# Expert queries of a PEER layer: one fp32 product each from the weights as loaded, in place of three products of high and low parts

## The chip, the cores and the metric

The program runs on one core of a Trainium2 chip. Its engines work side by side from their own instruction queues: TensorE (PE) multiplies, VectorE (DVE) and ScalarE (ACT) do elementwise work, GpSimd (POOL) issues the indirect gathers, SyncE (SP) issues the plain loads; semaphores join them. The metric is device microseconds of one execution; lower is better. All tensors are fp32.

## The reference, cut to what matters

Two transformer blocks on 256 tokens of width 1024. The change touches the last layer, an expert layer with 16384 experts, two tables of 1024-wide rows (`u`, `v`), 8 heads and 16 experts per head and token.

```
q = (h @ w_q).reshape(B, S, PEER_HEADS, 2, PEER_KEY_DIM)          # 1024 x 2048 weights
sc = jnp.einsum('bshpd,phnd->bshpn', q, keys)                     # 2 x 128 scores per head
v1, i1 = lax.top_k(sc[..., 0, :], 16);  v2, i2 = lax.top_k(sc[..., 1, :], 16)
...                                                               # best 16 of the 256 sums -> idx, gates
ue = jnp.take(u, it, axis=0)                                      # gathered rows of u
act = jax.nn.gelu(jnp.einsum('tkd,td->tk', ue, ht), approximate=False)
ve = jnp.take(v, it, axis=0)
return jnp.einsum('tk,tkd->td', gt * act, ve)
```

## The kernel before

**Weights.** Each matrix is cut into pieces of 1 MB, in the order of use (`weight_plan`). SP loads them into four places RAW. For each piece ACT (`hi`, L1214) writes the high part WH, rounded to fp32r, and DVE (`lo`, L1716) writes the low part WL = RAW - WH, 128x2048, and then the place in RAW may be loaded again. PE multiplies in fp32r: high by high, high by low, low by high (`mm3`). The last eight pieces are the query weights, one per head (`peer_q`). The activations, too, stand as XH and XL. `W`, `YY` and `WH`/`WL` are buffers of split weights.

**The end of the mixer.** `out_half(0, ..)` ends the first 128 tokens; DVE scales them (L2292), PE turns them round (L1082), ACT and DVE write XH and XL (`turn_half`). Then PE runs `query`: the queries of head 0 for half 0 (`first_query(0, 0)`: 16 pairs of a 128x128 weight tile and 128 columns, three products each), their scores, the rest of `out_half(1, ..)`, head 1 for half 0, and then half 1 of both heads. Heads 2 to 7 come as `query_tile(i, r)`, with all 256 tokens as columns: two tiles of 8 pairs each.

**The experts.** A "unit" is one head of one half of the tokens: its 16 experts are 16 "items" (256 in all). For item j, POOL issues a gather of 128 rows of `u` (one per token), and for item j - 8 one of `v` (512 gathers of 512 KB, L2612). DVE multiplies a u row with the token and sums (the "dot", L2451); every 8 items ACT takes the gelu and DVE the gate; ACT makes a diagonal matrix of 128 weights (L1674), PE multiplies it with the v rows and adds up in PSUM (two products of 512 columns, `item`). DVE's choice of the next unit's experts (`choose`, L2298 to L2404) lies between the dots.

**Slots.** The gathers land in 33 slots (`spots`) used in a ring: 13 at first, 12 more from item 64, 8 in RAW, two per place, as the places come free of the query weights ("lo" of pieces 4 to 7). `OPEN` says at which item a slot joins and what POOL waits for; later fills wait for the dot or the product (`v_mm`) that read the slot. `SCHEDULE` is one list that all engines follow: it says after which items a tile, the copy of its queries (`evict`), its scores, the copy of these (`keep`) and, in the kernel before, a `lo` come.

Of the kernel before, what the change touches and what calls it, by code (L numbers as in the profile page):

```python
# [126 lines left out]
def body(nc, ctx, A, out):  # L127
# [32 lines left out]
    NT = (XH[:, :, :], XL[:, :, :])  # L160
    ident, ones, negtri, negones, tri_le, tri_gt, bt_le, bt_gt = [cst[:, i, :] for i in range(8)]
# [127 lines left out]
    spots += [GS[:, i, :] for i in range(8, 20)]  # L289
    spots += [RAW[:, i // 2, D * (i % 2):D * (i % 2) + D] for i in range(8)]  # L290
# [16 lines left out]
    NSPLIT = len(plan) - 1  # L307
# [26 lines left out]
    SCHEDULE = [("query", 0), ("tile", (2, 0)), ("tile", (2, 1)), ("items", range(0, 5)), ("lo", 2), ("items", range(5, 7)),  # L334
                ("lo", 3), ("items", range(7, 8)), ("evict", 2), ("scores", 2), ("items", range(8, 9)), ("keep", 2)]
    j = 9
    for i in range(3, 8):
        t = 12 + 10 * (i - 3)
# [6 lines left out]
    Q = first["peer_q"] - 1  # L345
    OPEN = {s: (0, ("out1", 4 if s < 8 else 1)) for s in range(EARLY)}
# [15 lines left out]
    for j in range(256 + LAG):  # L362
        ring.extendleft(sorted((s for s in OPEN if OPEN[s][0] == j), key=lambda s: (s < 8, s), reverse=True))
# [24 lines left out]

    def pe_program():
# [684 lines left out]
        def turn_half(half):  # L1076
            for q in range(2):
# [7 lines left out]
                freed[i] = (S["turned"], 4 * TURN["peer"] + 2 * half + q + 1)  # L1085
# [40 lines left out]
        def query():  # L1126
            b01 = ring(0, 1)
            pe.wait_ge(S["xn"], 4)
            w0 = piece(8, ("pq_mm", 3))
# [5 lines left out]
            w1 = piece(8, ("pq_mm", 4))  # L1135
# [66 lines left out]
    def act_program():  # L1202
# [375 lines left out]
        def turn_half(half):  # L1578
            for q in range(2):
                act.wait_ge(pe.own, pe.nth("tr_half", 2 * half + q + 1))  # L1580
                nc.scalar.activation(XH[:, 4 * q:4 * q + 4, half * 128:half * 128 + 128],
                                     four(bank[at_bank["turn_half", half, q]]), ACT.Copy).then_inc(act.own, act.mark("tr_half"))
# [16 lines left out]
        hi()  # L1599
# [34 lines left out]
        def evict(i):  # L1634
# [4 lines left out]
            if i + 2 < 8:  # L1639
                hi()  # L1640
# [1063 lines left out]
```

## Time and profile before

| | us |
|---|---|
| runs | 1665.99 median (1664.35 to 1671.23, 3 runs) |
| profiled execution | 1665.4 |
| its span, first to last instruction | 1663.9 |
| first gather issued | 976.81 |
| last gather issued | 1643.61 |
| PE, DVE, ACT, POOL busy | 90%, 64%, 39%, 33% of the span |

The profiled execution is 1.5 us longer than its span, and 0.6 us under the median of the runs. The gathers move 268.47 MB of the 431.95 MB in the last 41% of the span. There the 16 DMA engines are busy nearly all the time, PE has long stretches in which it waits for data, and DVE is full only at the start. A share of busy time over the whole span says little here; the stretches are read one by one.

### The profile page before, as it was taken

What the parts mean: (1) busy time and instruction counts of PE and PEld (TensorE: products, weight loads), DVE (VectorE), ACT (ScalarE), POOL (GpSimd) and SP (SyncE); (2) the same over time, 40 slices, a digit from 0 to 9 for tenths busy, and PEclk for the clock granted to TensorE, in tenths of its full rate; (3) what the DMA queues carried; (4) which work ended last, traced back from release to release, by engine and by line L of the source; (5) the groups of instructions that cost most, each with busy time, mean ns of one, the idle gap of its engine ahead of it and who ended that gap; (6) DMA issues with size and microseconds to landing.
All of it is one profiled execution on the core that took longest, in us unless ns stands there. A gap on an engine that the chain in (4) does not pass through costs nothing.

```text
span 1663.9 us, 20481 instructions
## 1 busy us (share of the span) xinstructions
PE 1490.9 (90%) x8043; PEld 1100.5 (66%) x8043; DVE 1060.9 (64%) x1889; ACT 643.6 (39%) x1016; POOL 552.2 (33%) x607
## 2 busy tenths in 40 slices
PE   7999999999999999999999999998777777777776
PEld 7999898888888899998889886644222222222222
DVE  4655655677675555556655769776666667666655
ACT  5444343787354444444553534322222212222211
POOL 1000000311000000000010046777777776777774
PEclk9999999999999999999999999999999999999999
DMA  8555545334344355566444469999999999999997
GB/s 293 178 178 193 187 152 177 102 102 152 115 154 149 129 187 192 178 189 199 132 127 138 154 239 365 385 412 412 411 412 411 411 412 381 412 411 412 411 411 319
DMA packets 199945, 431.95 MB, mean 260 GB/s; under 512 B 20773, under 2 KB 114090, under 8 KB 199850
## 3 DMA queue, kind: packets, MB, share of 16 engines
q0 software_dynamic: 73728, 268.47, 40.5%
q1 hardware_dynamic: 123456, 159.92, 29.6%
q10 hardware_dynamic: 2666, 2.26, 0.5%
q8 instruction: 64, 1.05, 0.3%
q14 instruction: 31, 0.25, 0.0%
HBM read 429.55 MB, written 1.05 MB: 259 GB/s over the span
## 4 chain that ended last, share of the span: by engine, by line
PE 52%; POOL 17%; DVE 10%; DMA 9%; issue 7%; ACT 5%; ACTq 0%; DVEq 0%; POOLq 0%
PE ps L407 52%; POOL GS L2612 10%; POOL RAW L2612 5%; DVE WL L1716 3%; DMA GS<-in_peer_v_dram,AR 2%; ACT WH L1214 2%; DMA AR<-in_peer_v_dram,AR 2%; POOL AR L2612 2%; DMA RAW<-in_peer_v_dram,AR 2%; DMA RAW<-in_peer_u_dram,AR 1%; DMA GS<-in_peer_u_dram,AR 1%; DVE H L1758 1%; DVE XN L1753 1%; DVE XL L1772 1%; DVE AR L1980 0%
## 5 line engine op out<-in xcount | busy, mean ns | idle before, releaser
L1716 DVE TENSOR_TENSOR WL<-RAW,WH 128x2048 fp32r<-128x2048 f32 x143 | 327.9, 2293 | 232.1 <-ACT WH L1214 231.5
L407 PE MATMUL ps<-XH,WH 128*128 128x256 f32 (+1 forms) x1448 | 418.8, 289 | 12.3 <-DVE XL L1772 5.1
L407 PE MATMUL ps<-XL,WH 128*128 128x256 f32 (+1 forms) x1448 | 411.0, 284 | 0.0
L407 PE MATMUL ps<-XH,WL 128*128 128x256 f32 (+1 forms) x1448 | 410.9, 284 | 0.0
L407 PE MATMUL ps<-GS,AR 128*128 128x512 f32 x576 | 281.3, 612 | 81.4 <-DMA GS<-in_peer_v_dram,AR 70.3
L1214 ACT ACTIVATE WH<-RAW 128x2048 fp32r<-128x2048 f32 x137 | 262.4, 1915 | 181.7 <-PE ps L407 179.9
L407 PEld LDWEIGHTS ps<-XH,WH 128*128 128x128 f32 x1448 | 279.4, 193 | 21.0 <-issue 9.5
L407 PEld LDWEIGHTS ps<-XL,WH 128*128 128x128 f32 x1448 | 279.5, 193 | 3.2 <-issue 2.4
L407 PEld LDWEIGHTS ps<-XH,WL 128*128 128x128 f32 x1448 | 279.5, 193 | 0.0
L407 PEld LDWEIGHTS ps<-GS,AR 128*128 128x128 f32 x576 | 99.2, 190 | 259.5 <-issue 223.7
L2451 DVE CUSTOM_DVE_ANT_0 GS<-GS,ps 128x1024 f32<-128x1024 f32 x146 | 177.8, 1218 | 124.6 <-DMA GS<-in_peer_u_dram,AR 124.2
L2502 POOL TENSOR_TENSOR small<-small 128x1 f32<-128x1 f32 x28 | 15.4, 556 | 702.6 <-DVE small L1748 365.8
L407 PE MATMUL ps<-WH,YY 128*128 128x512 f32 x544 | 169.2, 392 | 1.6 <-DVE YY L1823 0.7
L2612 POOL DMA_INDIRECT GS<-in_peer_v_dram,AR x147 | 141.6, 963 | 45.5 <-issue 42.0
L2612 POOL DMA_INDIRECT GS<-in_peer_u_dram,AR x146 | 139.3, 954 | 51.4 <-issue 32.8
L407 PE MATMUL ps<-RAW,AR 128*128 128x512 f32 x248 | 119.5, 607 | 29.7 <-DMA RAW<-in_peer_v_dram,AR 25.5
L407 PE MATMUL ps<-AR 128*128 128x512 f32 (+8 forms) x556 | 125.6, 384 | 21.1 <-DMA AR<-in_peer_v_dram,AR 13.7
L407 PEld LDWEIGHTS ps<-AR 128*128 128x128 f32 (+3 forms) x556 | 73.4, 185 | 67.4 <-issue 48.5
L407 PEld LDWEIGHTS ps<-WH,YY 128*128 128x128 f32 x544 | 100.3, 188 | 22.7 <-issue 1.9
L1684 ACT ACTIVATE AR<-AR 128x8 f32<-128x8 f32 x32 | 6.7, 210 | 280.5 <-DVE AR L2451 280.5
L2451 DVE CUSTOM_DVE_ANT_0 RAW<-RAW,ps 128x1024 f32<-128x1024 f32 x62 | 75.4, 1217 | 54.2 <-DMA RAW<-in_peer_u_dram,AR 54.2
L407 PEld LDWEIGHTS ps<-RAW,AR 128*128 128x128 f32 x248 | 42.5, 189 | 101.4 <-issue 88.3
(372 smaller groups left out, 1988.9 us busy)
## 6 DMA issues: line engine op xcount, KB each, us to landing
RAW<-in_ffn_w_gu_dram SPq DMA_DIRECT2D x44, 1024.0 KB, 5.1
RAW<-in_w_in_dram SPq DMA_DIRECT2D x39, 1024.0 KB, 5.2
RAW<-in_ffn_w_down_dram SPq DMA_DIRECT2D x22, 1024.0 KB, 4.9
RAW<-in_w_out_dram SPq DMA_DIRECT2D x12, 1024.0 KB, 4.9
RAW<-in_xa_wkv_dram SPq DMA_DIRECT2D x8, 1024.0 KB, 5.3
RAW<-in_w_peer_q_dram SPq DMA_DIRECT2D x8, 1024.0 KB, 7.6
RAW<-in_xa_wq_dram SPq DMA_DIRECT2D x4, 1024.0 KB, 6.3
RAW<-in_xa_wo_dram SPq DMA_DIRECT2D x4, 1024.0 KB, 4.9
```

Of the source, the lines that this page charges most:

```text
L407: return nc.tensor.matmul(out_, lhsT, rhs, start=start, stop=stop, skip_group_check=True)
L1214: nc.scalar.activation(conv(0, k, kt), v, ACT.Copy).then_inc(act.own, act.mark("hi"))
L1684: nc.scalar.activation(un[n % 3]["g"][:, v], un[n % 3]["a"][:, v], ACT.Gelu).then_inc(act.own, act.mark("gelu"))
L1716: nc.vector.tensor_tensor(conv(1, k, kt), v, conv(0, k, kt).bitcast(F32), ALU.subtract).then_inc(S["lo"], 1)
L1753: nc.vector.tensor_tensor(XN[:, half, :], pair[half], GB[:, row % 2, :], ALU.mult).then_inc(S["post_g"], 1)
L1758: nc.vector.scalar_tensor_tensor(out=v, in0=XN[:, half, a:a + 512], scalar=rs[:, half:half + 1], in1=v, op0=ALU.mult, op1=ALU.add).then_in ...
L1772: ins = nc.vector.scalar_tensor_tensor(out=XL[:, c, :], in0=src, scalar=pg(gain, c), in1=h_, op0=ALU.mult, op1=ALU.subtract)
L2451: nc.vector.tensor_tensor_reduce(spots[s], spots[s], xn_ps[n // 8], 1.0, 0.0, ALU.mult, ALU.add, x["a"][:, kk:kk + 1]).then_inc(S["dot"], 1)
L2502: nc.gpsimd.tensor_tensor(dst, src, half_c[:, 0:1], ALU.pow).then_inc(S["rstd"], 1)
L2612: nc.gpsimd.indirect_dma_start(spots[s], None, table, bass.IndirectOffsetOnAxis(un[m % 3]["idx"][:, row % 16:row % 16 + 1], 0)).then_inc(S ...
```

## The change

The eight query pieces are no longer split. PE takes them as they were loaded, as fp32, with fp32 activations XF, in one product per pair (`mm` in place of `mm3`). `turn_half` writes XF: ACT the left four column blocks, DVE the right four, each straight from PSUM. The calls of `hi` and `lo` for these pieces are gone. Pieces 0 to 3 stay in RAW until their product is done; pieces 4 to 7 are loaded into the buffers WH and WL once the split pieces there have been used (4 and 5 after the last piece of the HGRN projection, 6 and 7 after the second part of `out_half(1, ..)`). The slots open by `pq_mm`, the end of a head's query product; 15 slots are there at first instead of 13. `SCHEDULE` moves the tiles: a tile every 11 items instead of every 10, tile 3 earlier. Three semaphores (`lb_max`, `rbc`, `gate_r`) are replaced by others with the same order of work.

```
-    spots = [GS[:, i, :] for i in range(8)]
+    spots = [GS[:, i, :] for i in (0, 1, 2, 3, 4, 5, 6, 7, 10, 11)]
...
-    SCHEDULE = [("query", 0), ("tile", (2, 0)), ("tile", (2, 1)), ("items", range(0, 5)), ("lo", 2), ("items", range(5, 7)),
-                ("lo", 3), ("items", range(7, 8)), ("evict", 2), ("scores", 2), ("items", range(8, 9)), ("keep", 2)]
+    SCHEDULE = [("query", 0), ("tile", (2, 0)), ("tile", (2, 1)), ("items", range(0, 6)), ("evict", 2), ("tile", (3, 0)),
+                ("scores", 2), ("items", range(6, 8)), ("keep", 2), ("tile", (3, 1)), ("items", range(8, 10)), ("evict", 3),
...
-    OPEN.update({s: (64, ("psc_mm", 10)) for s in range(EARLY, EARLY + 12)})
-    for i, j in enumerate((16, 24, 34, 44)):
-        OPEN.update({EARLY + 12 + 2 * i + r: (j, ("lo", Q + 4 + i + 1)) for r in range(2)})
+    for i, j in enumerate((12, 13, 16, 20, 30, 41, 52, 63)):
+        OPEN.update({EARLY + 2 * i + r: (j, ("pq_mm", i + 3)) for r in range(2)})
+    OPEN.update({EARLY + 16 + r: (64, ("pq_mm", 10)) for r in range(2)})
...
-                ins = mm3(bank[b][:, r * 256:r * 256 + 256], wcols(w, c, r * 128, 128), (XH[:, c, :], XL[:, c, :]),
-                          c == 0, c == 7)
+                ins = mm(bank[b][:, r * 256:r * 256 + 256], w[:, c, r * 128:r * 128 + 128], XF[:, c, :], c == 0, c == 7)
...
-            if what == "lo" or what == "keep" and n + 2 < 8:
-                lo()
...
+            if n >= PQ + 4:
+                i = n - PQ
+                sp.wait_ge(pe.own, pe.nth(*gone[in_turn[-2 if i < 6 else -1]]))
+                sp.wait_ge(S["raw%d" % s], raw_at[n - NRAW])
+                nc.sync.dma_start(QW[i].rearrange("p (c n) -> p c n", c=8), src).then_inc(S["raw%d" % s], 16)
+                return
```

POOL's queue, before, from the eleventh u row on (GS, AR, LB and RAW are where the slots lie; "waits dot" is the dot that read the slot, "waits tensor" a product of PE, "waits vector" the indices):

```order
L2612 DMA GS<-in_peer_u_dram,AR 128x1024
L2612 DMA AR<-in_peer_v_dram,AR 128x1024 [waits dot]
L2612 DMA AR<-in_peer_u_dram,AR 128x1024 [waits dot]
L2612 DMA AR<-in_peer_v_dram,AR 128x1024 [waits dot]
L2612 DMA AR<-in_peer_u_dram,AR 128x1024 [waits dot]
L2612 DMA LB<-in_peer_v_dram,AR 128x1024 [waits dot]
L2612 DMA GS<-in_peer_u_dram,AR 128x1024 [waits dot]
L2612 DMA GS<-in_peer_v_dram,AR 128x1024 [waits dot]
L2612 DMA GS<-in_peer_u_dram,AR 128x1024 [waits dot]
L2612 DMA GS<-in_peer_v_dram,AR 128x1024 [waits dot]
L2612 DMA GS<-in_peer_u_dram,AR 128x1024 [waits tensor]
L2612 DMA GS<-in_peer_v_dram,AR 128x1024 [waits dot]
```

The same place after the change:

```order
L2615 DMA GS<-in_peer_u_dram,AR 128x1024
L2615 DMA GS<-in_peer_v_dram,AR 128x1024
L2615 DMA GS<-in_peer_u_dram,AR 128x1024
L2615 DMA AR<-in_peer_v_dram,AR 128x1024 [waits dot]
L2615 DMA RAW<-in_peer_u_dram,AR 128x1024 [waits tensor]
L2615 DMA RAW<-in_peer_v_dram,AR 128x1024
L2615 DMA RAW<-in_peer_u_dram,AR 128x1024 [waits tensor]
L2615 DMA RAW<-in_peer_v_dram,AR 128x1024
L2615 DMA AR<-in_peer_u_dram,AR 128x1024 [waits dot]
L2615 DMA AR<-in_peer_v_dram,AR 128x1024 [waits dot]
L2615 DMA AR<-in_peer_u_dram,AR 128x1024 [waits dot]
L2615 DMA LB<-in_peer_v_dram,AR 128x1024 [waits dot]
```

Two more gathers need no slot to come free, four go to RAW on the queries of half 1, and the waits on dots and on the first v product stand later in the queue.

DVE's queue before, where the first unit's dots (ISA) and the choice for the second lie (`lo` is the 128x2048 row):

```order
L2306 MAX_INDEX AR<-AR 128x8 [waits vector]
L1716 TENSOR_TENSOR WL<-RAW,WH 128x2048 [waits scalar]
L2451 ISA GS,AR<-GS,ps 128x1024 [waits gather0]
L2451 ISA AR 128x1
L2384 TENSOR_SCALAR AR<-AR 128x16 [waits best]
L2385 TENSOR_SCALAR AR<-AR 128x16
L2387 CAST AR<-AR 128x32 [waits vector]
L2451 ISA GS,AR<-GS,ps 128x1024 [waits gather1]
L2451 ISA AR 128x1
L2391 TENSOR_TENSOR AR<-AR 128x512 [waits vector]
L1716 TENSOR_TENSOR WL<-RAW,WH 128x2048 [waits scalar]
L2451 ISA GS,AR<-GS,ps 128x1024 [waits gather2]
```

The same place after the change:

```order
L2313 MAX_INDEX AR<-AR 128x8 [waits vector]
L2458 ISA GS,AR<-GS,ps 128x1024 [waits gather0]
L2458 ISA AR 128x1
L2391 TENSOR_SCALAR AR<-AR 128x16 [waits best]
L2392 TENSOR_SCALAR AR<-AR 128x16
L2394 CAST AR<-AR 128x32 [waits vector]
L2458 ISA GS,AR<-GS,ps 128x1024 [waits gather1]
L2458 ISA AR 128x1
L2398 TENSOR_TENSOR AR<-AR 128x512 [waits vector]
L2458 ISA GS,AR<-GS,ps 128x1024 [waits gather2]
```

The dots and the choice keep their order; the long subtractions between them are gone.

## Rows read from the trace of the kernel before

**Rows 1.** Page, part 3: DMA queues, packets, MB, share of 16 engines.
```profile
q0 software_dynamic: 73728, 268.47, 40.5%
```

**Rows 2.** Stretches: us, busy of PE, PEld, DVE, ACT, POOL, PEclk, DMA share, GB/s.
```profile
965.00:979.00 14.00, 13.53 (x86) 12.05 (x85) 6.43 (x24) 4.16 (x6) 3.04 (x4) 1.00 0.00 2
979.00:981.00 2.00, 2.00 (x17) 1.88 (x17) 1.86 (x10) 1.22 (x2) 1.54 (x2) 1.00 0.62 127
1000.00:1045.00 45.00, 41.48 (x173) 26.59 (x173) 41.53 (x87) 18.94 (x38) 29.03 (x28) 0.92 0.97 364
1060.00:1095.00 35.00, 33.20 (x124) 18.13 (x123) 24.65 (x47) 12.73 (x30) 27.39 (x26) 1.00 1.00 386
1095.00:1385.00 290.00, 230.00 (x564) 90.62 (x563) 198.24 (x483) 64.49 (x171) 215.05 (x228) 1.00 1.03 411
1385.00:1400.00 15.00, 11.33 (x24) 3.81 (x23) 12.69 (x37) 4.82 (x11) 10.09 (x11) 1.00 0.89 324
```

**Rows 3.** POOL in order of time: start, us, what, idle before and its releaser.
```profile
976.81 2.80 POOL L2612 DMA_INDIRECT AR<-in_peer_u_dram,AR  x1 [10.36 <-DVE AR L2365]
1000.63 2.91 POOL L2612 DMA_INDIRECT LB<-in_peer_v_dram,AR  x1 [0.30 <-issue]
1009.59 1.15 POOL L2612 DMA_INDIRECT GS<-in_peer_u_dram,AR  x1 [2.79 <-DVE AR L2451]
1016.99 0.94 POOL L2612 DMA_INDIRECT GS<-in_peer_u_dram,AR  x1 [4.58 <-DVE AR L2300]
1035.92 2.36 POOL L2612 DMA_INDIRECT GS<-in_peer_v_dram,AR  x1 [0.30 <-issue]
1061.06 2.93 POOL L2612 DMA_INDIRECT RAW<-in_peer_u_dram,AR  x1 [0.30 <-PE ps L407]
1086.82 2.35 POOL L2612 DMA_INDIRECT RAW<-in_peer_v_dram,AR  x1 [0.30 <-issue]
1386.77 0.57 POOL L2502 TENSOR_TENSOR small<-small 128x1 f32<-128x1 f32 x1 [7.59 <-DVE small L1720]
```

**Rows 4.** DVE in order of time: three of seven low parts, first dot, second unit's index.
```profile
976.26 2.29 DVE L1716 TENSOR_TENSOR WL<-RAW,WH 128x2048 fp32r<-128x2048 f32 x1 [0.38 <-ACT WH L1214]
1000.45 2.27 DVE L1716 TENSOR_TENSOR WL<-RAW,WH 128x2048 fp32r<-128x2048 f32 x1
988.52 1.21 DVE L2451 CUSTOM_DVE_ANT_0 AR<-AR,ps 128x1024 f32<-128x1024 f32 x1
1011.84 0.18 DVE L2404 SCALAR_TENSOR_TENSOR AR<-AR 128x16 uint32<-128x16 f32 x1
1060.91 2.27 DVE L1716 TENSOR_TENSOR WL<-RAW,WH 128x2048 fp32r<-128x2048 f32 x1
```

**Rows 5.** Chain of waits: start, us from a gather's issue to its landing.
```profile
1086.82 7.02 DMA RAW<-in_peer_v_dram,AR
1642.36 12.08 DMA GS<-in_peer_v_dram,AR
```

**Rows 6.** PE in order of time: query, mixer and, out of their place, fp32 products.
```profile
965.07 0.27 PE L407 MATMUL ps<-XH,WH 128*128 128x128 f32 x1
965.18 0.27 PE L407 MATMUL ps<-XL,WH 128*128 128x128 f32 x1
974.05 0.39 PE L407 MATMUL ps<-YY,XH 128*128 128x512 f32 x1
1009.04 0.28 PE L407 MATMUL ps<-XH,WH 128*128 128x256 f32 x1
1009.16 0.28 PE L407 MATMUL ps<-XL,WH 128*128 128x256 f32 x1
538.40 2.13 PE L859 MATMUL ps<-cst,AR 128*128 128x128 f32 x16
540.47 7.17 PE L407 MATMUL ps<-AR 128*128 128x256 f32 x32
1018.29 3.60 PE L407 MATMUL ps<-AR 128*128 128x512 f32 x8
```

More of the change, by code:

```diff
@@ L285, in body @@
     diag = [a2(P) for _ in range(8)]
-    spots = [GS[:, i, :] for i in range(8)]
+    spots = [GS[:, i, :] for i in (0, 1, 2, 3, 4, 5, 6, 7, 10, 11)]
+    AFTER_OUT = len(spots)
     spots += [a2(D), ar(3072, D), ar(4096, D), ar(5120, D), LB[:, :, :].rearrange("p a b -> p (a b)")]
     EARLY = len(spots)
-    spots += [GS[:, i, :] for i in range(8, 20)]
-    spots += [RAW[:, i // 2, D * (i % 2):D * (i % 2) + D] for i in range(8)]
     assert at[0] <= 14604
@@ L306, in body @@
     MEM = first["mem"]
-    NSPLIT = len(plan) - 1
+    PQ = first["peer_q"]
+    NSPLIT = PQ - 1
     def load_of(k):
@@ L323, in before_in_buf @@
         return next((j for j in range(k - 1, -1, -1) if buf_of[j] == buf_of[k]), None)
+    QW = [RAW[:, (PQ + i) % NRAW, :] for i in range(4)]
+    QW += [GS[:, a + 2 * buf_of[k]:a + 2 * buf_of[k] + 2, :].rearrange("p a n -> p (a n)")
+           for k in in_turn[-2:] for a in (12, 16)]
+    spots += [v[:, D * r:D * r + D] for v in QW for r in range(2)]
+    spots += [GS[:, 8, :], GS[:, 9, :]]
     DVE_HI = range(first["w_in"] + 13, first["w_in"] + 19)
@@ L331, in body @@
     LAG = 8
-    SCHEDULE = [("query", 0), ("tile", (2, 0)), ("tile", (2, 1)), ("items", range(0, 5)), ("lo", 2), ("items", range(5, 7)),
-                ("lo", 3), ("items", range(7, 8)), ("evict", 2), ("scores", 2), ("items", range(8, 9)), ("keep", 2)]
-    j = 9
-    for i in range(3, 8):
-        t = 12 + 10 * (i - 3)
+    SCHEDULE = [("query", 0), ("tile", (2, 0)), ("tile", (2, 1)), ("items", range(0, 6)), ("evict", 2), ("tile", (3, 0)),
+                ("scores", 2), ("items", range(6, 8)), ("keep", 2), ("tile", (3, 1)), ("items", range(8, 10)), ("evict", 3),
+                ("items", range(10, 11)), ("scores", 3), ("items", range(11, 13)), ("keep", 3)]
+    j = 13
+    for i in range(4, 8):
+        t = 15 + 11 * (i - 4)
         SCHEDULE += [("items", range(j, t)), ("tile", (i, 0)), ("items", range(t, t + 2)), ("tile", (i, 1)),
@@ L387, in body @@
     GATES = {max(5, 16 * m - 18): m for m in range(1, 16)}
+    raw_n, raw_at = [0] * NRAW, []
+    for n, src in enumerate(plan):
+        raw_n[n % NRAW] += 64 if type(src) is tuple else 16
+        raw_at.append(raw_n[n % NRAW])
     def pe_program():
@@ L1128, in query @@
             pe.wait_ge(S["xn"], 4)
-            w0 = piece(8, ("pq_mm", 3))
+            w0 = query_w(0)
             first_query(0, 0, w0, b01)
@@ L1134, in query @@
             out_half(1, 3, True)
-            w1 = piece(8, ("pq_mm", 4))
+            w1 = query_w(1)
             first_query(1, 0, w1, b01)
@@ L1578, in turn_half @@
         def turn_half(half):
[L1579 to L1582, printed above, removed]
+            act.wait_ge(pe.own, pe.nth("tr_half", 2 * half + 1))
+            nc.scalar.activation(XF[:, 0:4, half * 128:half * 128 + 128], four(bank[at_bank["turn_half", half, 0]]),
+                                 ACT.Copy).then_inc(S["xf_act"], 1)
         def first_query(i, half):
@@ L2278, in turn_half @@
         def turn_half(half):
-            for q in range(2):
-                o = slice(half * 128, half * 128 + 128)
-                dve.wait_ge(act.own, act.nth("tr_half", 2 * half + q + 1))
-                nc.vector.tensor_tensor(XL[:, 4 * q:4 * q + 4, o], four(bank[at_bank["turn_half", half, q]]),
-                                        XH[:, 4 * q:4 * q + 4, o].bitcast(F32), ALU.subtract).then_inc(S["turned"], 1)
-        lo()
+            dve.wait_ge(pe.own, pe.nth("tr_half", 2 * half + 2))
+            nc.vector.tensor_copy(XF[:, 4:8, half * 128:half * 128 + 128],
+                                  four(bank[at_bank["turn_half", half, 1]])).then_inc(S["xf_dve"], 1)
         dve.wait_ge(S["row0"], 48)
```

50 lines of the change are left out of this document (21 added, 29 removed).

## Prediction

> **What bounds the kernel now.** I read the page's DMA part, then the stretches of the end, POOL's order of time, DVE's beside it, the chain of waits, and PE's order of time last.
>
> The gathers are 268.47 MB [rows 1]. From 1095 to 1385 the DMA engines move 411 GB/s at a share of 1.03 [rows 2]: transfers set the pace, at 524.3 KB / 411 = 1.275 us a gather. POOL, where nothing stops it, issues one in 0.94 + 0.30 = 1.24 us [rows 3], slightly less, so the lag from issue to landing grows, from 7.02 us at 1087 to 12.08 us at 1642 [rows 5]. PE and DVE wait for data by then. So the end is: start of the stream, plus bytes over rate, plus what the stream loses. A change can gain only by an earlier start, fewer lost microseconds, or bytes taken out.
>
> Losses before: the DMA engines move nothing from 965 to 979 [rows 2]. From 1000 to 1045 they move 364 GB/s: (411 - 364) / 411 x 45 = 5.1 us lost. From 1060 to 1095, 386 GB/s: 2.1 us. From 1385 to 1400, 324 GB/s: 3.2 us. The last follows POOL's wait of 7.59 us for the first half's mean square [rows 3], which the change leaves in its place.
>
> The two losses before 1095 have two causes in POOL's rows. One is slots: POOL waits 2.79 and 4.58 us before two gathers, 0.30 being usual: 2.49 + 4.28 = 6.8 us [rows 3]. DVE is busy 41.53 of 45 us there [rows 2]: dots, the choice of experts, and four low parts of 2.3 us. The other cause is the issue itself: five gathers take 2.80, 2.91, 2.36, 2.93 and 2.35 us, not 0.94 [rows 3]. The three that I show begin inside a low part on DVE (976.26, 1000.45, 1060.91) and end 0.8 to 1.1 us after it: 1000.45 + 2.27 = 1002.72, the issue ends at 1003.54 [rows 3, 4]. The extra is 1.86 + 1.97 + 1.42 + 1.99 + 1.41 = 8.65 us. The other two I count as the same.
>
> The Trainium skill, "SBUF — State Buffer", section "SBUF: two separate sides", has a rule for this: VectorE and GpSimd hold one port pair by an exclusive lock for a whole instruction, and DVE takes it also with two SBUF inputs. The low part has two. By that rule all five vanish with the low parts, and the dots, which have one input in PSUM, lock nothing; the trace agrees.
>
> **The change part by part.**
>
> *The start of the stream.* The first gather waits for DVE's first choice, which waits for the queries of head 0 [rows 3]. Those are 48 fp32r products at a pitch of 965.18 - 965.07 = 0.112 us: 5.4 us [rows 6]. Now they are 16 fp32 products. Eight such (16 records) take 2.13 us with a tail of 0.27, so 0.248 each: 4.0 us. Gain 1.4 us. ACT and DVE write XF side by side rather than one after the other, but PE has mixer products to do meanwhile: nothing. Then the issue itself is 1.86 us shorter. First data 3.3 us earlier.
>
> *POOL.* Low parts gone: 8.65 - 1.86 = 6.8 us of issue. Slot waits: 6.8 us, if the slots keep up (below). POOL as a whole: 3.3 + 6.8 + 6.8 = 16.9 us.
>
> *Weight bytes in the stream.* Before, pieces 5, 6 and 7 follow low parts at 976, 1000 and 1006, so 3 x 1.05 MB / 411 = 7.7 us of the stream is theirs. Now 4 and 5 go out after the last RAW piece, near 957 to 965, where they meet no gather. Pieces 6 and 7 wait for the second part of `out_half(1, ..)`, which ended at 974.05 [rows 6], now 972.6. They need 5.1 us and a start of 1 to 2 us, so end near 979, while the gathers' data, which began near 979.4 (127 GB/s on average from 979 to 981 [rows 2]), begins at 976.1: 3.0 us overlap. Gain 7.7 - 3.0 = 4.7 us.
>
> *The stream.* Start 3.3, losses 5.1 + 2.1, weights 4.7: 15.2 us. POOL's 16.9 is more, so the transfers bind from the start and this sum counts. The two sums aren't added.
>
> *Do the slots keep up?* DVE first. Its first dot came at 988.52, and stands behind the second half's turn. That comes 1.4 us earlier with the start and 1.4 with the query product of head 1; the shared write of XF takes off 0.7 more (half of a copy and the DVE part behind it): 3.5 us, to 985. From there the index of unit 1 took 1011.84 - 988.52 = 23.3 us, with two low parts of 2.27 [rows 4]: now 18.8, at 1003.8. POOL wants it for its 25th gather, at 975.4 + 0.8 + 24 x 1.25 = 1006. Met with 2 us. Later dots are wanted 8 us and more after they are there.
>
> PE: heads 0 and 1, four products of which each is 1.4 us shorter, end some 6 us earlier, near 995. A tile of 16 pairs with 256 columns was 48 x 0.120 = 5.8 us [rows 6]. The fp32 one: 16 products (32 records) in 7.17 us less the tail of 0.3, 0.43 to 0.448 each: 7.0 us. So heads 2 and 3 and their scores take 15 us, and the first v product ends near 1012. POOL wants it for its 31st gather, at 1013.7. That is the tightest place: 2 us. After it a v row costs PE 3.60 / 2 = 1.8 us against 2.55 us per item, 0.75 left, and 11 items leave 8.3 us for 7.7 us of tile and scores. By the slots the later products are wanted 5 to 9 us after they end. Six tiles at +1.2 us are 7 us more of PE, hidden in these margins; without them 7 us would come back.
>
> The clock: the granted clock averages 0.92 of 2.4 GHz from 1000 to 1045 [rows 2], so 3.6 us are lost there to the 1.2 GHz level, after PE had waited in turn for ACT and DVE. If that stays, tiles 2 and 3 end 1 to 3 us late, and POOL waits 0 to 2 us. Taken: 1.2 us.
>
> A second rule speaks against the change. The Trainium skill, "FP8 and Floating Point Precision", section "TensorE Precision Notes", gives true fp32 four passes. Against three products of one pass, a tile would cost a third more, 7.7 us. Rows 6 say 0.43 to 0.448 against 0.36, a fifth to a quarter more. By the rule the tile phase gets 4 us more than by the rows, all within the margins but for the tight place.
>
> *Bounds.* DVE's and PE's share: 0 to 6.8 us of waits come back. Overlap of the weights: 0 (all before the first data) to 5.1. An fp32 product of 256 columns with weights from RAW, which no row shows: 0.40 us (the nearest row, less 10%) to 0.9 (twice it, all at 1.2 GHz); I take the row. XF copies: no cost seen. Outside this end nothing moves.
>
> Sum: 15.2 - 1.2 = 14.0 us. The profiled execution was 1665.4: 1651.4. The median stood 0.6 us over it: **1652.0 us**.
>
> **The rivals.**
>
> *A, the stream starts well and loses again (0.20).* PE's first v product or DVE's index is late, and POOL waits 4 to 8 us as now, only elsewhere. For it: margins of 2 us, worked out over many steps. Against it: 15 slots instead of 13, RAW four items sooner. Time: 1652 + 6 = 1658.
>
> *B, more than forecast (0.12).* Pieces 6 and 7 land before the gathers flow, and no clock is lost: 1665.99 - 15.2 - 3.0 = 1648. POOL's 16.9 us then bounds it, at 1649.
>
> *C, PE becomes the bound, slower than before (0.05).* Fp32 products hold PE at 1.2 GHz through the tile phase. A v row then costs 3.6 us against 2.55 and a tile 14. Each us at the low level takes 0.5 us; after margins of 2 to 9 us POOL waits one for one. Slower than before from 14 + 9 = 23 us of delay, that is 46 us at the low level in the 120 us from 995; all of it at 1.2 GHz gives 60 - 9 - 14 = 37 us more: 1703. Against it: from 1060 to 1385, with fp32 products throughout, the granted clock is 1.00 [rows 2]. This is also what four passes would lead to if they came with the low clock.
>
> *D, nothing gained (0.08).* The long issues aren't DVE's doing and stay, the lag absorbs the rest, and the weights just move. The gain is then the start, 1.4 us, and some of the slot waits: 1662.
>
> **How the numbers follow.** The forecast has 0.55. Its own range, from the bounds of overlap and waits, is 1648.5 to 1656. The range at 8 in 10 takes in B and most of A: 1647 to 1661. No change means within 0.5%, 8.3 us, about what a measurement of this kernel can tell: 1657.7 to 1674.3. Faster: forecast, B and half of A, 0.55 + 0.12 + 0.11 = 0.78, and 0.02 for a D that keeps more. Same: the rest of A, D, and a C that is small: 0.16. Slower: 0.04.
>
> **What would show it.** Right: first gather near 975.4, issued in 0.94 us; no gather over 1.3 us to 1095; no wait for a slot over 2 us; 405 GB/s or more from 985 to 1095; POOL's last issue near 1627, last landing near 1640; lag growing from the first gathers on; tiles of about 7 us. Wrong: issues of over 2 us with no low part beside them (the lock), POOL waiting for PE at the 31st gather or after (A), the granted clock below 0.9 from 1000 to 1095 with PE late (C), GB/s at 411 throughout but a later end (bytes or rate misjudged).

## The result and the profile after

The kernel after takes 1649.47 us (median of 4 runs, 1648.51 to 1649.87), the kernel before 1665.17 (4 runs, 1661.45 to 1671.23): a ratio of 0.9903, 95% interval 0.9884 to 0.9922. The forecast was 1652.0 us, with a range of 1647 to 1661. The profiled execution is 1649.16 us, its span 1647.8: 16.2 us less than before. The times of the kernel before spread widely, and the longest go with a low granted clock over the whole span (in 23 further executions, the four over 1668 us have 0.991 to 0.993, the others 0.994 to 0.998), while the four of the kernel after lie within 1.4 us at 0.997 to 0.998.

The same stretches as [rows 2] (columns as there), the line of 981 to 1000 added:

```profile
965.00:979.00 14.00, 13.53 (x84) 11.89 (x83) 7.25 (x35) 3.27 (x5) 3.92 (x7) 1.00 0.57 176
979.00:981.00 2.00, 2.00 (x20) 1.95 (x18) 1.09 (x2) 1.37 (x5) 1.57 (x2) 1.00 1.08 383
981.00:1000.00 19.00, 17.15 (x118) 15.65 (x117) 18.32 (x55) 3.73 (x10) 14.65 (x16) 1.00 1.03 413
1000.00:1045.00 45.00, 45.00 (x157) 27.57 (x156) 34.50 (x92) 15.90 (x40) 34.34 (x36) 1.00 1.03 413
1060.00:1095.00 35.00, 35.00 (x111) 19.62 (x110) 27.45 (x68) 12.05 (x33) 26.47 (x29) 1.00 1.03 411
1095.00:1385.00 290.00, 229.72 (x504) 86.88 (x503) 198.10 (x482) 66.44 (x177) 213.44 (x226) 1.00 1.02 408
1385.00:1400.00 15.00, 10.45 (x23) 3.71 (x22) 7.57 (x13) 0.00 (x0) 11.34 (x13) 1.00 1.03 412
```

The stream runs at 411 to 413 GB/s from 981 to 1095. Before it had 364 and 386 there. The one large loss left is POOL's wait for the first half's mean square, which now falls before 1385 and pulls that stretch to 408. PE is busy for all 45 us from 1000, at a granted clock of 1.00, where before it was 0.92.

POOL in order of time, against [rows 3]: the first gather, the one that wants the index of unit 1 (1005.78), the one that wants the first v product (1013.28), the longest issue, and the wait for the mean square.

```profile
974.72 1.19 POOL L2615 DMA_INDIRECT AR<-in_peer_u_dram,AR  x1 [9.10 <-DVE AR L2340]
1005.78 0.94 POOL L2615 DMA_INDIRECT RAW<-in_peer_u_dram,AR  x1 [0.30 <-issue]
1013.28 0.94 POOL L2615 DMA_INDIRECT GS<-in_peer_u_dram,AR  x1 [0.30 <-PE ps L423]
1019.85 1.44 POOL L2615 DMA_INDIRECT GS<-in_peer_v_dram,AR  x1 [0.30 <-issue]
1370.82 0.57 POOL L2505 TENSOR_TENSOR small<-small 128x1 f32<-128x1 f32 x1 [8.45 <-DVE small L1730]
```

No issue is over 1.44 us and no slot is waited for: 0.30 us stands before each gather. The issue of 1.44 us begins inside a DVE product with both inputs in SBUF (it is part of `choose`):

```profile
1019.79 0.69 DVE L2403 TENSOR_TENSOR AR<-AR 128x512 f32<-128x512 f32 x1
```

The product ends at 1019.79 + 0.69 = 1020.48, the issue at 1021.29, 0.81 us later. The ten other issues of 1.16 to 1.44 us between 1000 and 1600 do the same: each begins inside such a product or sum (of 128x512, in one case 128x256) and ends 0.81 or 0.82 us after it. So the hold that the low parts caused is still in the kernel after, only shorter. DVE and PE, against [rows 4] and [rows 6]: first dot, index of unit 1; the query of head 0, all 16 pairs of head 2, half of those of head 3, the first v products.

```profile
983.91 1.21 DVE L2458 CUSTOM_DVE_ANT_0 AR<-AR,ps 128x1024 f32<-128x1024 f32 x1
1004.46 0.18 DVE L2411 SCALAR_TENSOR_TENSOR AR<-AR 128x16 uint32<-128x16 f32 x1
```

```profile
964.44 3.73 PE L423 MATMUL ps<-GS,RAW 128*128 128x128 f32 x32
993.20 7.07 PE L423 MATMUL ps<-GS,RAW 128*128 128x256 f32 x32
1004.45 3.62 PE L423 MATMUL ps<-GS,RAW 128*128 128x256 f32 x16
1007.91 5.31 PE L423 MATMUL ps<-GS,AR 128*128 128x512 f32 x12
```

The chain of waits, against [rows 5]: the lag from issue to landing grows from early on, and falls back once, at the wait for the mean square.

```profile
1157.27 9.97 DMA GS<-in_peer_u_dram,AR
1350.21 14.66 DMA LB<-in_peer_u_dram,AR
1385.72 6.43 DMA GS<-in_peer_v_dram,AR
1626.28 12.10 DMA RAW<-in_peer_v_dram,AR
```

The last landing is at 1626.28 + 12.10 = 1638.38; before it was 1642.36 + 12.08 = 1654.44 [rows 5]. This is the gain of 16 us. What the plain queue moves between 976 and 1640 (packets, MB, share), first of the kernel before, then of after:

```profile
q1 hardware_dynamic: 3264, 3.67, 1.7%
```

```profile
q1 hardware_dynamic: 1481, 1.86, 0.8%
```

That is 1.81 MB less, or 4.4 us at 411 GB/s.

### The profile page after: what moved, and what is told of

Same layout as the page of the kernel before. It is cut to its first block, busy times and chain, and to the rows that moved or that the text cites. A ratio compares the mean times of both kernels' runs of the same rounds, so it can differ in the third digit from the quotient of the medians.

```text
span 1647.8 us, 20127 instructions
## 1 busy us (share of the span) xinstructions
PE 1484.6 (90%) x7883; PEld 1094.6 (66%) x7883; DVE 1041.2 (63%) x1879; ACT 628.3 (38%) x1006; POOL 545.0 (33%) x607
## 4 chain that ended last, share of the span: by engine, by line
PE 55%; POOL 13%; DMA 11%; DVE 10%; issue 6%; ACT 5%; ACTq 0%; DVEq 0%; POOLq 0%
PE ps L423 54%; POOL GS L2615 7%; DMA GS<-in_peer_u_dram,AR 4%; POOL RAW L2615 3%; DVE WL L1726 3%; ACT WH L1230 2%; DMA GS<-in_peer_v_dram,AR 2%; POOL AR L2615 2%; DMA RAW<-in_peer_u_dram,AR 2%; DMA RAW<-in_peer_v_dram,AR 2%; DMA LB<-in_peer_u_dram,AR 1%; DVE GS L2458 1%; DVE H L1768 1%; DVE XN L1763 1%; DVE XL L1782 0%
## 5 line engine op out<-in xcount | busy, mean ns | idle before, releaser
L1726 DVE TENSOR_TENSOR WL<-RAW,WH 128x2048 fp32r<-128x2048 f32 x135 | 309.6, 2293 | 230.9 <-ACT WH L1230 230.5
L423 PE MATMUL ps<-XH,WH 128*128 128x256 f32 x1288 | 369.7, 287 | 9.7 <-DVE XL L1782 4.9
L423 PE MATMUL ps<-XL,WH 128*128 128x256 f32 x1288 | 366.0, 284 | 0.0
L423 PE MATMUL ps<-XH,WL 128*128 128x256 f32 x1288 | 365.9, 284 | 0.0
L1230 ACT ACTIVATE WH<-RAW 128x2048 fp32r<-128x2048 f32 x129 | 247.2, 1916 | 180.4 <-PE ps L423 178.6
L423 PEld LDWEIGHTS ps<-XH,WH 128*128 128x128 f32 x1288 | 248.3, 193 | 15.2 <-issue 6.6
L423 PEld LDWEIGHTS ps<-XL,WH 128*128 128x128 f32 x1288 | 248.4, 193 | 0.7
L423 PEld LDWEIGHTS ps<-XH,WL 128*128 128x128 f32 x1288 | 248.3, 193 | 0.0
L423 PE MATMUL ps<-AR 128*128 128x512 f32 (+8 forms) x540 | 118.7, 378 | 20.8 <-DMA AR<-in_peer_v_dram,AR 13.4
L423 PE MATMUL ps<-WL,YY 128*128 128x512 f32 x272 | 106.0, 390 | 0.0
```

The source lines that it names most:

```text
L423: return nc.tensor.matmul(out_, lhsT, rhs, start=start, stop=stop, skip_group_check=True)
L1230: nc.scalar.activation(conv(0, k, kt), v, ACT.Copy).then_inc(act.own, act.mark("hi"))
L1726: nc.vector.tensor_tensor(conv(1, k, kt), v, conv(0, k, kt).bitcast(F32), ALU.subtract).then_inc(S["lo"], 1)
```

## The experiments

Each was timed beside the kernel before on the same chip; a ratio is to that kernel. The kernel after stands at 0.9903 in this measure. It was not timed again beside the variants, so a difference to its 1649.47 us is one between separate measurements; the kernel before had medians of 1664.96 to 1665.32 us in them, against 1665.17 beside the kernel after. Runs 2 to 12 are built from the kernel after.

**1. Is it the lock of one instruction?** From the kernel before:

```
+            if k >= first["peer_q"] - 1:
+                for q in range(8):
+                    ins = nc.vector.tensor_tensor(conv(1, k, kt)[:, q, :], v[:, q, :], ..., ALU.subtract)
```

> Made from the kernel before; it computes the same. The eight low parts of the query weights, one subtraction of 128x2048 each (2.3 us), become eight subtractions of 128x256 in a row. Theory (a gather's issue on POOL is held up until the one DVE instruction that runs beside it has ended, then takes about 0.8 us): an issue can now be held by one short subtraction at a time only, so the five issues of 2.4 to 2.9 us before 1095 fall below 1.5 us, and the stretches from 1000 to 1095 get back a part of the 8.65 us of issue: 1659 to 1664 against 1665.4 (the slot waits stay, DVE is 1 to 3 us slower over all by the starts of 56 more instructions). Rival 1 (the sheer load of two engines on the same memory holds the issue, whatever the instruction's length): the issues stay above 2 us, 1665 to 1668. Rival 2 (a held issue gets no turn between subtractions that follow each other): the same long issues as before.

Measured: 1663.26 us, ratio 0.9997 (0.9982 to 1.0012). DVE and POOL beside each other:

```profile
1059.77 2.75 DVE L1718 TENSOR_TENSOR WL<-RAW,WH 128x256 fp32r<-128x256 f32 x8
```

```profile
979.00 1.46 POOL L2618 DMA_INDIRECT AR<-in_peer_u_dram,AR  x1 [0.30 <-issue]
1005.24 0.94 POOL L2618 DMA_INDIRECT GS<-in_peer_u_dram,AR  x1 [4.02 <-DVE AR L2457]
1011.18 1.15 POOL L2618 DMA_INDIRECT GS<-in_peer_u_dram,AR  x1 [3.27 <-DVE AR L2457]
1016.31 1.02 POOL L2618 DMA_INDIRECT GS<-in_peer_u_dram,AR  x1 [2.31 <-PE ps L407]
1060.05 0.95 POOL L2618 DMA_INDIRECT RAW<-in_peer_u_dram,AR  x1 [0.30 <-issue]
1061.30 1.04 POOL L2618 DMA_INDIRECT RAW<-in_peer_v_dram,AR  x1 [0.30 <-issue]
```

A gather issued wholly beside eight short subtractions takes 0.95 us, where [rows 3] has 2.93 beside one long one. No issue before 1095 is over 1.5 us. Of the nine that begin inside a row of eight subtractions, seven take 0.94 to 1.04 us; the very first gather takes 1.27, and the one at 979.00 takes 1.46 and ends 0.81 us after the last subtraction of its row (976.88 + 2.77 = 979.65). The same bytes read and written on DVE don't hold the issue for 2 us and more, so the first rival falls, and the second too. The time hardly followed, though: the slot waits went from 2.79 and 4.58 to 4.02, 3.27 and 2.31. Much of what POOL gained at the issue it then waited for DVE and PE. The stretches from 1000 to 1045 and from 1060 to 1095 have 381 and 412 GB/s in place of 364 and 386, which is 1.9 + 2.2 us, and the profiled execution is 1662.32 us, 3.1 under the one before. Over all executions the kernel is no faster by an amount that can be told.

**2 and 3. Locks, or just DVE's time?** From the kernel after, at seven places (in the first choice, after items 4, 6, 8, 18, 28, 38); first the lock, then the same time without it:

```
+            nc.vector.tensor_tensor(JA[...], k, k, ALU.subtract)            # k in SBUF, 128x2048
...
+            for q in range(2):
+                ins = nc.vector.tensor_scalar(JA[...], pair[3], 1.0, None, ALU.mult)      # PSUM, 128x1024
```

> Made from the kernel after; seven extra subtractions on DVE of 128x2048 with both inputs in SBUF, whose results nobody reads, stand where the low parts stood (one in the first choice of experts, then after items 4, 6, 8, 18, 28 and 38). Theory (POOL and DVE time of the low parts is what cost 8.65 us of issue and 6.8 us of slot waits): issues of 2 to 3 us come back beside them, five to seven of them, some 8 us of issue; DVE's index for unit 1 comes 4 to 6 us later (1009 to 1011, wanted at 1006), so a slot wait of 2 to 5 us comes back too. With the start 1.9 us later, and the lag absorbing part of it: 1654 to 1661 against 1649.5. Rival (only the weight bytes and the start mattered, the transfers bind anyway): 1649 to 1652.

> Made from the kernel after; at the seven places of the run with extra subtractions stand instead two DVE copies each of 128x1024 from PSUM, whose results nobody reads: about the same DVE time (2 x 1.1 us), but one input and that in PSUM. Theory (the lock belongs to an operation with two inputs in SBUF): no issue of a gather over 1.5 us, only DVE's lateness is left, 1650 to 1655. Rival (any busy DVE holds the issue): issues of 2 to 3 us as in the run with the subtractions, and the same time as it.

Measured: 1659.19 us, 0.9963 (0.9950 to 0.9975), with locks; 1651.83 us, 0.9919 (0.9899 to 0.9939), without. With locks, DVE and then POOL:

```profile
1001.76 2.29 DVE L2451 TENSOR_TENSOR JA<-XN 128x2048 bf16<-128x2048 f32 x1
1007.92 2.29 DVE L2451 TENSOR_TENSOR JA<-XN 128x2048 bf16<-128x2048 f32 x1
```

```profile
1002.08 2.80 POOL L2626 DMA_INDIRECT RAW<-in_peer_v_dram,AR  x1 [0.30 <-issue]
1008.17 2.86 POOL L2626 DMA_INDIRECT AR<-in_peer_u_dram,AR  x1 [0.30 <-DVE AR L2411]
```

1001.76 + 2.29 = 1004.05, and the issue ends at 1004.88, 0.83 later. For the second it is 1010.21 and 1011.03. Without the lock:

```profile
1002.22 2.36 DVE L2451 TENSOR_SCALAR JA<-ps 128x1024 bf16<-128x1024 f32 x2
```

```profile
1009.17 0.94 POOL L2627 DMA_INDIRECT RAW<-in_peer_u_dram,AR  x1 [3.21 <-PE ps L423]
```

There is no long issue, and one wait of 3.21 us. That the copies are shorter, 1.18 us each, isn't the reason: by the 0.8 us of run 2 a gather that began inside one of them could still be held up to 2 us, and every one of them but the very first (1.19 us, as in the kernel after) took 0.94 or 0.95. So of the 9.7 us that the seven subtractions give back, 2.4 are DVE's time and 7.3 the lock. One expectation missed: with the locks no slot wait came back. POOL was held up itself, by 10.9 us of extra time in the seven issues beside the subtractions, and so wanted its slots later.

**4. The same locks late.** After items 68 to 118:

> Made from the kernel after; six of the extra subtractions stand after items 68, 78, 88, 98, 108 and 118, when gathers already wait 9 us and more in their queue. Theory (the stream of transfers sets the end, and POOL's lead absorbs a late issue): the issues beside them take 2 to 3 us again, 6 to 12 us of POOL time in all, yet GB/s stays at 405 or more and the end moves by less than 2 us: 1649 to 1652. Rival (POOL's issue is what bounds, at 1.24 to 1.25 us a gather against 1.275 us of transfer): each us of issue is a us at the end, 1656 to 1661.

Measured: 1652.98 us, 0.9922 (0.9901 to 0.9943): 3.5 us over the kernel after, above the theory's 1652 and below the rival's 1656. The profiled execution is the longest of the six, 1654.68. Six issues of 1.96 to 2.98 us come back. Stretches, first of the kernel after, then of this one:

```profile
1170.00:1300.00 130.00, 99.10 (x204) 34.43 (x203) 89.96 (x220) 30.24 (x78) 98.52 (x104) 1.00 1.03 412
```

```profile
1170.00:1300.00 130.00, 94.25 (x193) 32.53 (x192) 95.65 (x214) 27.25 (x72) 100.72 (x97) 1.00 1.00 385
```

Chain and POOL of this run:

```profile
1151.61 6.78 DMA GS<-in_peer_u_dram,AR
1278.38 6.13 DMA RAW<-in_peer_v_dram,AR
```

```profile
1376.64 0.57 POOL L2514 TENSOR_TENSOR small<-small 128x1 f32<-128x1 f32 x1 [2.31 <-DVE small L1730]
```

About 6.1 to 6.8 us is the lag of a gather that queues behind nothing. The kernel after had 9.97 at 1157, so only some 3.5 us were in stock; the six late issues, 9.8 us of extra time, used that up, and the transfers lost (412 - 385) / 412 x 130 = 8.5 us (405 GB/s or more was expected). POOL's wait for the mean square then fell from 8.45 to 2.31 us, and the stretch from 1370 to 1380 has 411 GB/s where the kernel after has 290, so 2.9 us came back there. 8.5 - 2.9 = 5.6 us is what separates the two profiled executions (1654.68 and 1649.16: 5.5). "Transfers bind" holds with a margin of 1.275 to 1.25, no more.

**5. Weight bytes in the stream.**

```
+                sp.wait_ge(pe.own, pe.nth("pq_mm", 3 if i < 6 else 4))
```

> Made from the kernel after; it computes the same. The last four query pieces are loaded later: 4 and 5 only after the third query product, 6 and 7 after the fourth, so that 4.2 MB go out while the gathers flow, one piece more than in the kernel before. Theory (the transfers bind from 985 on, so bytes in the stream cost bytes over rate, 4.2 MB / 411 = 10.2 us, less what no longer stands ahead of the first gathers, about 2 us, and less a wait of PE for the late pieces that changes nothing): 1655 to 1658 against 1649.5, with 405 GB/s or more up to 1045. Rival 1 (POOL's issue and the slots bound that stretch, the bytes fill gaps): 1649 to 1651. Rival 2 (the late pieces make tiles 2 to 5 late, POOL waits for the RAW slots and for the first v product): waits of 5 us and more on PE's products, 1660 to 1670.

Measured: 1660.68 us, 0.9970 (0.9960 to 0.9981), 11.2 us more, with no gather waiting over 1 us from 1000 on. 4.2 MB are 10.2 us: bytes cost at least their full price in this stream. The time is above the 1658 of the theory, and the rate below its 405 GB/s: 381 from 981 to 1000 and 399 from 1000 to 1045, where the kernel after has 413. That is 1.5 + 1.5 = 3.0 us lost while weights and gathers run together, at a DMA share of 1.01 and 1.04. With them the sum comes out: 10.2 + 3.0, less the 2 us for pieces no longer in the way of the first gathers, is 11.2.

**6. PE's margin.** Each query tile's products twice (`for c in list(range(8)) * 2`):

> Made from the kernel after; each query product of heads 2 to 7 is done twice (the second pass starts its sum anew, so the result is the same), which takes PE from 7 to 14 us a tile, 42 us more in all, of which 14 us stand ahead of the first v product. It is also what the tiles would take with PE at its 1.2 GHz level throughout. Theory of the prediction (the first v product ends about 2 us before POOL wants its slot, later products have 5 to 9 us): POOL waits for the first v product some 20 us, for tiles 2 and 3 and the third copy, then the stream loses again as each tile of 14 us stands beside 11 items of 0.75 us spare each, 14 - 9 = 5 us for four or more tiles: 1649.5 + 25 to 45, 1675 to 1695, slower than the kernel before. Rival (PE has more room than worked out): under 1665.

Measured: 1675.90 us, 1.0061 (1.0047 to 1.0076), slower than before. POOL, first two of six waits:

```profile
1012.95 0.94 POOL L2615 DMA_INDIRECT RAW<-in_peer_u_dram,AR  x1 [6.83 <-DVE AR L2411]
1024.51 0.94 POOL L2615 DMA_INDIRECT GS<-in_peer_u_dram,AR  x1 [4.38 <-PE ps L423]
```

The six (6.83, 4.38, 5.05, 1.97, 6.41, 6.42) are 31.1 us, less 0.3 each 29.3; the end moved by 26.4. 42 us more of PE cost 26: margins of about 16 us over six tiles. Of the 20 us expected ahead of the first v product, the first two waits are 10.6. So rival C's arithmetic was a real way to lose; the low clock that it starts from was not seen.

**7. The start.** Head 0's first query product twice:

> Made from the kernel after; only the query product of head 0, half 0, is done twice (16 more fp32 products of 128 columns, 3.7 us by the records of the first one; the result is the same). The first gather then comes 3.7 us later. Theory (the end is the start of the stream plus bytes over rate): the end moves one for one, 1652.5 to 1653.5 against 1649.5, and the later waits stay as they are. Rival (slack further on takes it up, above all POOL's wait of 8.45 us for the first half's mean square): less than 1.5 us at the end.

Measured: 1652.98 us, 0.9925 (0.9909 to 0.9941). The first gather is issued at 978.59, 3.87 us later than in the kernel after, and the end comes 3.5 us later. The start counts nearly one for one.

**8. The wait for the mean square.** `FINISH = {150: 0, 154: 1, 168: 2, 176: 3}`:

> Made from the kernel after; it computes the same. The first half's mean square and what follows it (stages 2 and 3 of the end of that half) are moved from items 157 and 162 to items 168 and 176, so that POOL comes to it when DVE has long written it, and does not stand for 8.45 us between two gathers at 1362. Theory (that wait empties the queue of transfers, 290 GB/s from 1370 to 1380, some 3 us lost, and the lag that the wait uses up is then there later too): no wait of POOL over 1 us after 1000, 405 GB/s or more from 1360 to 1400, the end 3 to 4 us earlier: 1645.5 to 1646.5. Rival (POOL is the bound before and after by its 1.25 us a gather, all 8.45 us of the wait count): 1641 to 1643. Rival 2 (nothing, since slots of the ring are late by then): 1649.

Measured: 1649.60 us, 0.9906 (0.9890 to 0.9922): nothing, rival 2's time, but not for its reason. The wait is gone and POOL's last issue is at 1618.65, not 1627.53. From 1370 to 1380 the stream has 410 GB/s instead of 290. The end, first of the kernel after, then of this run:

```profile
1630.00:1635.00 5.00, 3.79 (x9) 1.36 (x8) 2.57 (x2) 0.97 (x3) 0.00 (x0) 1.00 1.03 410
1635.00:1640.00 5.00, 3.64 (x8) 1.06 (x6) 2.78 (x3) 0.00 (x0) 0.00 (x0) 1.00 0.35 138
```

```profile
1630.00:1635.00 5.00, 3.89 (x9) 1.36 (x8) 2.57 (x2) 0.91 (x3) 0.00 (x0) 1.00 0.57 229
1635.00:1640.00 5.00, 3.48 (x8) 1.06 (x6) 2.94 (x3) 0.00 (x0) 0.00 (x0) 1.00 0.05 20
```

```profile
1617.39 20.82 DMA RAW<-in_peer_v_dram,AR
```

1617.39 + 20.82 = 1638.21, as in the kernel after (1638.38). Most of the 16 DMA engines finish some 4 us earlier, and a share of 0.05, about one engine of 16, goes on to 1638. This fits that the gap at 1370 had stopped the quick engines and not the one that was behind, so that closing it gave the end nothing; the profile doesn't tell the engines apart, so it isn't shown.

**9. The early RAW slots.** The first eight RAW slots join at items 16, 24, 34, 44, as before:

> Made from the kernel after; it computes the same. The first eight slots in RAW join the ring at items 16, 24, 34 and 44, as in the kernel before, instead of at 12, 13, 16 and 20. Theory of the prediction (the early slots are needed: with 15 slots alone POOL comes back to dots and to the first v product before they are done): POOL waits for a dot or the first v product between 1000 and 1020, 5 to 9 us in all, GB/s under 390 from 1000 to 1045, the end 3 to 6 us later than 1649.5: 1653 to 1656. Rival (DVE without low parts is early enough that two more slots than before do): waits under 2 us, 1649 to 1651.

Measured: 1650.32 us, 0.9907 (0.9891 to 0.9923). POOL waits 2.07 us for the first v product, once. The rival holds: the early slots are worth about 1 us at most.

**10. Why is one DMA engine late?** From run 8, eight reached waits before the products of items 60 to 235 on PE:

> Made from the run with the later sums (stages 2 and 3 at items 168 and 176), with eight waits on a semaphore that has long been reached ahead of the products of each item from 60 to 235 on PE: some 1,400 more instructions, nothing else; it computes the same. In the run with the later sums POOL issued its last gather 9 us earlier than in the kernel after, and the end stayed; in its last 5 us the DMA engines moved 12 to 37 GB/s, about one sixteenth of 411, so one engine was that far behind the others. Theory (the packets of kind instruction, 16 KB each, 12 of them between 976 and 1640 at 1.0 to 1.1 us, all fall on one DMA engine, and the end follows that one): about 5.5 more such packets, 3.5 us (at the engine's share of 25.7 GB/s) to 6 us later, with a longer tail of about 27 GB/s: 1653 to 1656. Rival (the engines are just unequal, and 90 KB more bytes are 0.2 us over all): 1649 to 1650.5, tail as before.

Measured: 1649.92 us, 0.9907 (0.9892 to 0.9923). Only 3 more instruction packets came (15 for 12), of which the theory makes at least 3 x 0.64 = 1.9 us; 0.3 came. The one late engine isn't explained by code; what explains it stays open.

**11 and 12. Both back, then the slots too.** Run 2's subtractions, pieces 5 to 7 loaded late (`pq_mm` 2 and 4); then run 9's slots besides.

> Made from the kernel after: the seven extra subtractions of the run with locks, and the last three query pieces (5, 6, 7) loaded after the second and fourth query products, 3.1 MB in the stream as in the kernel before. Theory (between 1000 and 1060 the locks leave the transfers idle for about 7 us, so that weight bytes partly fill gaps: the two costs, 9.7 us for the locks, about 8 for three of the four late pieces that cost 11.2, do not add up): 1661 to 1664. Rival (they add up): 1666 to 1668.

> Made from the run with both back (seven extra subtractions, three late query pieces, 1659.1 us, no slot wait of POOL over 0.3 us), with the first eight RAW slots joining at items 16, 24, 34 and 44 besides. It is then the kernel before but for the 15 first slots instead of 13, the shorter query products, the order of the tiles and the place of the last pieces. Theory (the early slots are what keeps a late DVE and a late PE from stopping POOL; with DVE early they cost 0.7 us, with DVE held up by the subtractions they cost more): POOL waits 4 to 7 us for dots or the first v product between 1005 and 1025, 1662.5 to 1665. Rival (their price does not depend on DVE): 1659.5 to 1660.5, waits under 3 us. What is then still missing to 1665.2 is the later start, 1.7 us, and the two slots less.

Measured: 1659.07 us, 0.9960 (0.9947 to 0.9973), and 1658.97 us, 0.9964 (0.9950 to 0.9977). Both theories fell: with the locks there, 3.1 MB of weights cost nothing, and the late slots cost nothing either. From 1000 to 1020, first run 2, then run 11:

```profile
1000.00:1020.00 20.00, 20.00 (x77) 13.13 (x76) 19.55 (x44) 6.29 (x15) 16.13 (x13) 1.00 0.88 291
```

```profile
1000.00:1020.00 20.00, 20.00 (x78) 13.11 (x77) 19.55 (x45) 6.29 (x15) 16.20 (x13) 1.00 1.04 399
```

POOL is the same in both; the weights fill just the gaps that it leaves. The costs are those of two resources side by side, POOL's issue and the transfers, and the larger counts, not the sum.

Run 12 is still 6.2 us from the kernel before (1665.2), and its slot waits did not come back. One reason can be read from the traces. The wait of 4.58 us before the gather at 1016.99 is the first v product: this gather is the one whose slot waits for PE in the queue of the kernel before, and the releaser that its row names, a DVE instruction, is not the one it waited for. Before, ACT and PE in order of time, then PE's clock in that stretch:

```profile
1010.81 1.90 ACT L1214 ACTIVATE WH<-RAW 128x2048 fp32r<-128x2048 f32 x1
1013.06 5.40 PE L407 MATMUL ps<-GS,AR 128*128 128x512 f32 x8 [0.87 <-ACT AR L1674]
1013.00:1016.50 3.50, 3.44 (x4) 1.39 (x5) 3.47 (x6) 2.48 (x9) 0.00 (x0) 0.53 1.07 384
```

PE in run 12:

```profile
1008.27 5.31 PE L423 MATMUL ps<-GS,AR 128*128 128x512 f32 x12
```

Before, the diagonal matrix that PE needs stood behind a high part on ACT until 1012.61, for which PE waited 0.87 us, and the first v product then ran at a granted clock of 0.50 to 0.58 and took 3.6 us (the 5.40 are two rows of v, and the second takes 1.8), to about 1016.7. In run 12 it started 4.8 us earlier, at a granted clock of 1.00 from 1000 to 1045, and took 1.8. The high parts on ACT and the clock are two things that no run put back. So run 12 differs from the kernel before in more than its expectation lists.

## Why the prediction was right, step by step

- *What bounds.* This was right: a start moved by 3.9 us gives 3.5 (run 7), 4.2 MB give 11.2 (run 5). The margin over POOL is thin, as the rates of 1.275 and 1.24 said, and run 4 showed what that means: a stock of 3.5 us.
- *The start.* The forecast was 3.3 us. The first issue ends at 974.72 + 1.19 = 975.91, before at 976.81 + 2.80 = 979.61 [rows 3]: 3.7. The 0.4 us between is less than executions differ by: the same code up to there issues its first gather at 974.20 in run 8 and at 976.41 in run 9. The query product took 3.73 us, forecast 4.0. The size of this term is good to about 1 us.
- *Losses of 5.1 and 2.1 us.* Both are gone, with 413 and 411 GB/s. That one long DVE instruction with two SBUF inputs holds the issue is shown by runs 1 to 3. By the Trainium skill, "SBUF — State Buffer", section "SBUF: two separate sides", a DVE instruction with two SBUF inputs keeps off a GpSimd instruction that reads SBUF, and for the whole instruction. The prediction left out the condition on the read; an indirect gather reads its indices from SBUF (AR in its rows), so it is met. Run 3, with one input in PSUM, and run 1, with short instructions, agree.
- *Slot waits of 6.8 us.* Gone, as forecast, but partly for another reason. The prediction names only DVE's load for the two waits. The larger one, 4.58 us, was the first v product, and of it 0.9 us are PE's wait for ACT behind a high part and 1.8 us the low clock (above). The change took both away: the high parts by design and the low clock as a consequence that the prediction did not count on. That part was luck.
- *Weights.* 4.7 us forecast; 4.4 by the bytes. But run 11 shows that this is no gain of its own while the long issues are there. In the kernel before, too, these bytes lay in stretches where POOL left gaps, so the same should hold there; it was not tried in that kernel. The terms are right as an account of the stream after, and wrong as prices of single edits. Of the 6.2 us from run 12 (1659.0) back to 1665.2 the earlier start of run 12 is 1.7 us (975.10 for 976.81). The rest goes with the slot waits of 6.8 us, which did not return: DVE's index came at 1007.75 there and at 1011.84 before [rows 4], 13 first slots were 15, the high parts on ACT were gone and the clock was full. How much each of these saved wasn't tried.
- *Slots.* DVE's index was forecast for 1003.8 and came at 1004.46. Two errors cancel in it: the first dot came at 983.91, not 985, and from there the index took 20.6 us, not 18.8. The first v product starts at 1007.91 and takes 1.8 us for a row, so it is done about 1010 against "near 1012" and wanted at 1013.3. A tile took 2 x 3.62 less the tails, 6.9 us, against 7.0. Nothing was waited for. The early RAW slots, which the prediction counted among what avoids rival A, hardly mattered (run 9).
- *The step that was off: the clock and a late PE, 1.2 us.* It was taken that the 0.92 of [rows 2] would repeat. It didn't: before, PE was busy for 41.48 of the 45 us and waited for ACT and DVE in between; now it is busy for all 45, and the granted clock was 1.00. Of the difference of 2.2 us (16.2 against 14.0) this is 1.2. The rest is the 0.4 us of the start and the mean square's loss, which went from 3.2 us to (411 - 408) / 411 x 290 = 2.1, less the 0.3 of the weights. These shares are read from one execution each, and the start alone differs by more than 1 us between executions; only the clock and the missing wait are plain to see.
- *Four passes.* A tile takes 6.9 us and not 7.7. What fails here is not the four passes that the Trainium skill gives, "FP8 and Floating Point Precision", section "TensorE Precision Notes", but the prediction's step from them to 7.7, which took a whole fp32r product of 0.120 us as the price of one pass. In cycles of 2.4 GHz, 0.43 us are 4.0 for each of 256 columns, and 0.120 us are 1.1. So the measured duration of an fp32 product agrees with four passes, if one takes a cycle a column, and an fp32r product costs a little more than one. The 0.7 us a tile would have been hidden by the margins of run 6 anyway.
- *Rivals.* B came nearest: no clock was lost, and its 1648 is 1.5 us off, while the forecast's 1652.0 is 2.5 off. B's other half, pieces 6 and 7 landing before the gathers, didn't happen: a DMA share of 1.08 at 383 GB/s from 979 to 981 shows them side by side. A and D did not occur. C's condition, PE at the low clock, did not occur either; run 6 shows only that a PE of half the speed in the tiles would be slower than before.

No variant beats the kernel after by what can be told; run 8 equals it.

## What to carry to other kernels

Where GpSimd issues gathers, look for VectorE instructions with two SBUF inputs beside each issue of unusual length. Shortening them frees the issue, but this only pays if the slots it then wants are ready. Before adding up losses, ask which of them share the same gap: bytes and stalls that lie in parallel are worth the larger, and taking out both may be needed to gain either. Closing a gap in the mean rate of a transfer stream need not move the end: look at how the last few microseconds of the stream run out. And a releaser that a row names is a guess: where the program's own queue says that a gather waits for PE, look at PE and its clock.

## What the runs showed of the hardware

- An indirect gather whose issue began beside a 128x2048 subtraction with two SBUF inputs (2.29 us) ended its issue 0.81 to 0.83 us after it in six of seven cases of run 2 (1.06 in the first). In the kernel after, the same 0.81 or 0.82 us follow operations of 0.69 us (128x512). Issued beside eight subtractions of 128x256 it took 0.94 to 1.04 us in seven of nine cases of run 1 (1.27 and 1.46 in the others); beside copies from PSUM (run 3) 0.94 or 0.95.
- An fp32 product takes 0.43 us with 256 columns and 3.73 / 16 = 0.23 us with 128, against 0.36 and 0.34 for three fp32r ones [rows 6]. So it is the cheaper way at 128 columns and the dearer one at 256.
- PE's granted clock fell below 1.00 before where PE had waited for ACT and DVE (0.53 from 1013.0 to 1016.5, after a wait of 0.87 us), and averaged 1.00 from 1000 to 1045 where PE had no gap.
- While plain 1 MB weight loads and gathers run together, the 16 DMA engines are full at less than 411 GB/s: 383 at a share of 1.08 from 979 to 981 in the kernel after, 399 at 1.04 from 1000 to 1045 in run 5.
- The DMA engines don't finish together: at the end of run 8, about one went on to 1638 after the others (a share of 0.08 and 32 GB/s from 1634 to 1638). Why it is behind, the runs leave open.
